# A hybrid decoder step on one core: the sample's state space beside the last projection units, attention's constants awaited where they are read, and the first expert tile's lookup in four parts

## The reference, cut to what matters

```python
proj = rmsnorm(h, g_mix) @ w_in                       # 1024 -> z, xbc, dt, q, k, v
xc = silu(causal_dwconv(concat(conv_buf, xbc), conv_w) + conv_b)
y, ssm_final = ssd_chunked(xs * dt, adt, b, c, ssm0)  # prompt: 8 chunks of 128; sample: one chunk of 4
y_ssm = grouped_rmsnorm((y + d_skip * xs) * silu(z)) * g_ssm_norm
o = diff_attention(q, k_all, v_all, pos0, lam, rel_bias)   # sample: against 2048 cached tokens in pages
h = h + concat(y_ssm, rmsnorm(o, g_diff_norm) * (1 - lam_init)) @ w_out
q = rmsnorm(h) @ w_query                              # 8 heads, two halves of 128
s1, i1 = top_k(q[..0] @ keys0.T, 16); s2, i2 = top_k(q[..1] @ keys1.T, 16)
sc, pos = top_k(s1[:, None] + s2[None, :], 16); idx = (i1 * 128 + i2)[pos]
h = h + sum_k softmax(sc)_k * gelu(u[idx_k] . x) * v[idx_k]      # 128 experts a token
h = h + (p_l @ w_ple) * sigmoid(rmsnorm(h) @ w_ple_gate); y = rmsnorm(h, g_final)
```

## Time and profile before

| | |
|---|---|
| three runs | 3808.51, 3808.66, 3820.09 us; median 3808.66 |
| profiled execution | 3804.01 us; span on the core 3802.4 us |
| PE busy | 2278.3 us (60%), 9714 instructions |
| DVE busy | 2223.9 us (58%), 5285 |
| ACT busy | 1166.0 us (31%), 3659 |
| POOL busy | 1277.7 us (34%), 1247 |
| moved by DMA | 1260.74 MB, 332 GB/s over the span |
| chain that ended last, by engine | DMA 39%, PE 15%, issue 7%, DVE 6%, ACT 6%, POOL 4% |
| the same chain's largest line | the gathers of L2488: 38% |

### The profile page before, as it was taken

How to read it: one execution, slowest core, us unless ns; L and a number is a source line. 1 busy time by engine, 2 the same in 40 slices (tenths; PEclk the granted TensorE clock), 3 DMA queues, 4 the chain that set the end, 5 groups by cost and what they waited for, 6 DMA issues and landing times.

```text
span 3802.4 us, 33311 instructions
## 1 busy us (share of the span) xinstructions
PE 2278.3 (60%) x9714; PEld 775.3 (20%) x9714; DVE 2223.9 (58%) x5285; ACT 1166.0 (31%) x3659; POOL 1277.7 (34%) x1247
## 2 busy tenths in 40 slices
PE   7999934869355456355545635544564563466667
PEld 3555421435011011011101101100110110022211
DVE  4235143543768756855875685586578557645553
ACT  3122113431232422242242223224223322434443
POOL 0000012310244444444434444444444443433332
PEclk9899966989667567566656757666675765677778
DMA  3211027963499999999999999999999999999995
GB/s 102 69 51 57 20 72 266 344 223 121 198 421 421 421 420 421 413 415 421 412 413 419 420 414 410 421 416 407 421 418 413 419 420 412 406 362 391 382 397 213
DMA packets 214609, 1260.74 MB, mean 332 GB/s; under 512 B 27670, under 2 KB 30315, under 8 KB 79043
## 3 DMA queue, kind: packets, MB, share of 16 engines
q0 software_dynamic: 165008, 1147.82, 73.8%
q1 hardware_dynamic: 42122, 93.59, 7.0%
q10 hardware_dynamic: 7296, 17.21, 1.2%
HBM read 1238.80 MB, written 24.25 MB: 332 GB/s over the span
## 4 chain that ended last, share of the span: by engine, by line
DMA 39%; PE 15%; issue 7%; DVE 6%; ACT 6%; POOL 4%; ACTq 1%; POOLq 0%; DVEq 0%; SPq 0%
DMA ex_ring<-in_expert_uv,ex_idx_cur 38%; PE ex_acc L2650 6%; PE ex_pk L2312 4%; POOL ex_ring L2488 4%; DVE ex_ring L2598 2%; ACT ex_diag L2540 2%; ACT ex_coef L2534 2%; PE ex_pt L1896 1%; PE ex_pk L1918 1%; PE ex_pk L2161 1%; PE ex_pk L2324 1%; DMA ex_ring<-in_expert_uv,ex_idx_few 1%; ACT ex_act_out L2531 1%; DVE ex_work L2059 1%; DVE ex_work L2052 1%
## 5 line engine op out<-in xcount | busy, mean ns | idle before, releaser
L2598 DVE CUSTOM_DVE_ANT_0 ex_ring<-ex_ring,ex_rows 128x1024 f32<-128x1024 f32 x1056 | 1292.5, 1225 | 923.0 <-DMA ex_ring<-in_expert_uv,ex_idx_cur 880.4
L2488 POOL DMA_INDIRECT ex_ring<-in_expert_uv,ex_idx_cur x1024 | 1131.9, 1105 | 1690.6 <-PE ex_acc L2650 1370.2
L2650 PE MATMUL ex_acc<-ex_ring,ex_diag 128*32 128x512 f32 x4224 | 866.4, 892 | 1138.9 <-ACT ex_diag L2540 1138.4
L2531 ACT ACTIVATE ex_act_out<-ex_dots 128x2 f32<-128x2 f32 x528 | 108.0, 205 | 1746.8 <-DVE ex_dots L2598 1746.3
L2650 PEld LDWEIGHTS ex_acc<-ex_ring,ex_diag 128*32 128x32 f32 x4224 | 105.8, 129 | 1835.5 <-ACT ex_diag L2540 1762.6
L2540 ACT ACTIVATE ex_diag<-ex_pick_row,ex_coef 128x32 f32<-128x32 f32 x1056 | 283.2, 315 | 49.4 <-ACT ex_coef L2534 1.1
L2534 ACT ACTIVATE ex_coef<-ex_act_out,ex_gate_cur 128x1 f32<-128x1 f32 x1024 | 246.6, 288 | 16.7
L1918 PE MATMUL ex_pk<-ex_w,ex_aT 128*128 128x512 f32 x512 | 250.2, 631 | 0.5 <-DVE ex_aT L1967 0.5
L293 PE MATMUL pj_bank<-pj_aT,pj_wbuf 128*128 128x512 f32 x512 | 226.4, 598 | 0.4 <-ACT pj_aT L408 0.4
L2312 PE MATMUL ex_pk<-ex_w,ex_aT 128*128 128x512 f32 (+1 forms) x288 | 151.2, 677 | 47.0 <-issue 45.2
L1896 PE MATMUL ex_pt<-ex_wo,ex_aT 128*128 128x512 f32 x256 | 131.4, 657 | 5.7 <-ACT ex_aT L1932 5.7
(11 more groups left out here) (377 smaller groups left out, 2497.0 us busy)
## 6 DMA issues: line engine op xcount, KB each, us to landing
at_ring<-in_cache_kT POOLq DMA_DIRECT2D x64, 256.0 KB, 6.4
at_ring<-in_cache_kT SPq DMA_DIRECT2D x64, 256.0 KB, 8.9
at_ring<-in_cache_v SPq DMA_DIRECT2D x64, 256.0 KB, 9.4
at_ring<-in_cache_v POOLq DMA_DIRECT2D x64, 256.0 KB, 6.2
ex_ring<-in_expert_uv,ex_idx_cur POOLq DMA_INDIRECT x1024, 13.3
pj_wbuf<-in_w_in SPq DMA_DIRECT2D x6, 2048.0 KB, 8.5
ex_ring<-in_w_queryT ACTq DMA_DIRECT2D x4, 2048.0 KB, 23.5
pj_front<-in_x_all SPq DMA_DIRECT2D x8, 512.0 KB, 4.4
```

What stands on the lines that cost most here:

```text
L2488: pool.indirect_dma_start(ring[:, c % RING, :], None, t["expert_uv"], bass.IndirectOffsetOnAxis((idx_cur[k % 2] if k < LAST else idx_few)[ ...
L2531: act.activation(act_out[:, half, :], dots[:, half, :], ACT.Gelu).then_inc(gelu_done, 1)
L2598: dve.tensor_tensor_reduce(out=u, in0=u, in1=rows[:, j, :], scale=1.0, scalar=0.0, op0=ALU.mult, op1=ALU.add, accum_out=dots[:, q % HALVES ...
L2650: mm = pe.matmul(acc[n][quarter(j), :], diag[:, q % HALVES, p, :], ring[:, c % RING, D + n * 512:D + (n + 1) * 512], start=False, stop=las ...
```

## The change

1. `ssd` is gone. The sample's state space is spread over the last units of the projection: from unit `FEW` = 52 each engine runs one step (`few_tensor`, `few_scalar`, `few_vector`) behind its part of the unit, in tiles that the projection has done with. SP loads its inputs behind the weights (`few_loads`) and stores the results (`few_stores`). ACT's two convolution copies stand behind k's "few" unit, and the prompt's last `out_vector` in unit 52's step.

```diff
+    FEW = SSD_AT + PT * PHASES
+        def few_stores(sp):
+            sp.wait_ge(f_y_up, 1 + G)
+            sp.dma_start(t["mix"][SEQ:SEQ + DEC, 0:D_SSM], f_y).then_inc(f_stored, 16)
+            for b in range(DEC_B):
+                sp.wait_ge(f_added, b + 1)
+                sp.dma_start(t["ssm_s"][b], f_state[:, b, :]).then_inc(f_stored, 16)
...
+        def few_new(pe, b):
+            if b >= 2:
+                pe.wait_ge(f_added, b - 1)
+            for i in range(G):
+                part = slice(i * HALF, (i + 1) * HALF)
+                mm = pe.matmul(q_new[b % 2][:, part], f_xc[:, D_SSM + i * NS:D_SSM + (i + 1) * NS], f_xdm[:, b, part],
+                               start=True, stop=True)
+            mm.then_inc(f_new, 1)
...
+        def few_tensor(pe, at):
...
+            elif at == 9:
...
+                pe.wait_ge(f_s_in, 32)
+                pe.wait_ge(f_own_up, 1)
+                for i in range(G):
+                    for b in range(DEC_B):
+                        mm = pe.matmul(q_o[:, i * HALF:(i + 1) * HALF], f_cTm[:, b, i, :],
+                                       f_state[:, b, i * HALF:(i + 1) * HALF], start=(b == 0), stop=(b == DEC_B - 1))
+                mm.then_inc(f_off, 1)
+                pe.wait_ge(f_el_up, 1)
+                for b in range(2):
+                    few_new(pe, b)
...
+            elif at >= 10:
+                for b in (2, 3) if at == 10 else range(4, DEC_B):
+                    few_new(pe, b)
...
+        def few_vector(dve, v, at):
...
+            elif at == 10:
+                dve.wait_ge(f_off, 1)
+                v.step(dve.tensor_tensor(heads(f_y), heads(q_o), wide(f_eac[:], few_head), ALU.mult))
+                dve.wait_ge(f_diag, 1)
...
+                dve.tensor_tensor(f_y, f_y, f_z, ALU.mult).then_inc(f_y_up, 1)
+                for b in range(2):
+                    few_add(dve, v, b)
+            elif at == 11:
+                for b in range(2, DEC_B):
+                    few_add(dve, v, b)
...
                 for c in range(2, len(CHUNKS)):
                     weights(c)
+                few_loads(sp)
+                few_stores(sp)
...
+                    if n >= FEW:
+                        few_tensor(pe, n - FEW)
...
-        ssd(nc, t, sample=True)
```

```diff
+            if U == 0:
+                pe.wait_ge(val_in, 16)
...
+            if U < HD:
+                dve.wait_ge(bias_in[U], 16)
...
+        def sample_start(dve, v):
+            dve.wait_ge(sel_in, 16 * 3)
+            dve.wait_ge(consts, 16 * 2)
...
+            dve.wait_ge(s_bias_in, 16 * DEC_S)
...
+                for tok in range(DEC_S):
+                    act.dma_start(s_bias[tok::DEC_S, :],
+                                  bass.AP(t["line"].tensor, X_OFF - PAST - tok, [[0, 8], [LINE, HD], [1, PAST + DEC_S]])
+                                  ).then_inc(s_bias_in, 16)
...
+                    if U == 3:
+                        sample_start(dve, v)
```

```diff
+        def rest_vector(dve, v):
+            for n in range(1, PAIRS):
+                dve.wait_ge(scored, n + 1)
+                for step, _ in enumerate(search(dve, n, v, pk[n], ranked, n + 1, 0)):
+                    if n >= 2 and step == 6:
+                        first_divide(dve, v, n - 1)
+                    yield
+                yield from first_found(dve, v, n)
+            yield from few_vector(dve, v)
...
+                for n in range(4):
+                    src = t["w_queryT"][4 * n * P:4 * (n + 1) * P, :].rearrange("(c p) d -> p c d", p=P)
+                    sp.dma_start(wqT[:, 4 * n:4 * n + 4, :], src).then_inc(wq_in[n], 16)
...
+                        if k == 0 and i % QUADS == 0:
+                            pool.wait_ge(idx0, GRP * GRP * (i // QUADS + 1))
...
-                for n in range(4):
-                    src = t["w_queryT"][4 * n * P:4 * (n + 1) * P, :].rearrange("(c p) d -> p c d", p=P)
-                    act.dma_start(wqT[:, 4 * n:4 * n + 4, :], src).then_inc(wq_in[n], 16)
...
+                rest = rest_vector(dve, v)
+                for _ in range(4):
+                    next(rest)
+                rows_vector(dve, 0, 0)
+                first_divide(dve, v, 0)
+                for j in range(1, GRP):
+                    for _ in range(3):
+                        next(rest)
                     rows_vector(dve, 0, j)
```

More of the change, by code:

```diff
@@ L2123, in few_vector @@
         def few_vector(dve, v):
[L2124 removed]
             dve.wait_ge(few_scored, 1)
[L2126 removed]
+            for step, _ in enumerate(search(dve, 0, v, pk[0], few_ranked, 1, 0)):
+                if step == 6:
+                    first_divide(dve, v, PAIRS - 1)
+                yield
             v.settle()
             dve.tensor_copy(idx_few[:], idx_f[:, 0:QUADS]).then_inc(few_idx, 1)
[L2129 removed]
             dve.tensor_scalar(neg[:, 0:2], best[:, 0:2, 0], -1.0, None, ALU.mult).then_inc(few_negated, 1)
@@ L2137, in few_scalar @@
         def few_scalar(act):
-            yield from pause(33)
             act.wait_ge(few_ranked, 1)
@@ L2144, in few_scalar, with first_found @@
                                accum_out=total[:, h:h + 1]).then_inc(few_grown, 1)
+        def first_found(dve, v, n):
+            v.settle()
+            dve.tensor_scalar(neg[:, 2 * n:2 * n + 2], best[:, 2 * n:2 * n + 2, 0], -1.0, None, ALU.mult).then_inc(negated0, 1)
+            at, end = n * QUADS, (n + 1) * QUADS
+            for j in range(GRP):
+                for q in range(GRP):
+                    dve.tensor_copy(idx_cur[0][quarter(q), at + j:end:GRP], idx_f[quarter(j), at + q:end:GRP]).then_inc(
+                        idx0, 1)
+                yield
@@ new lines, in first_divide, with first_grow @@
+        def first_divide(dve, v, n):
+            two = slice(2 * n, 2 * n + 2)
+            dve.wait_ge(grown0, 2 * (n + 1))
+            v.step(dve.reciprocal(total[:, two], total[:, two]))
+            dve.tensor_tensor(gate_f[:, two], gate_f[:, two], wide(total[:, two], [P, 2, TOPK]), ALU.mult).then_inc(
+                divided0, 1)
+        def first_grow(act, n):
+            act.wait_ge(ranked, n + 1)
+            act.wait_ge(negated0, n + 1)
+            for h in range(2 * n, 2 * n + 2):
+                act.activation(gate_f[:, h, :], best[:, h, :], ACT.Exp, bias=neg[:, h:h + 1],
+                               accum_out=total[:, h:h + 1]).then_inc(grown0, 1)
@@ L2148, in experts, with rest_scalar @@
+        def rest_scalar(act):
+            yield from pause(5)
+            for n in range(1, PAIRS):
+                first_grow(act, n)
+                yield from pause(9)
+                yield from first_gates(act, n)
+                yield from pause(4)
+            few_scalar(act)
         wqT = ring[:].rearrange("p r d -> p (r d)").rearrange("p (c d) -> p c d", d=D)
@@ L2580, in _ @@
                     pass
-                for j in range(groups_of(0)):
+                dve.wait_ge(scored, 1)
+                for _ in search(dve, 0, v, pk[0], ranked, 1, 0):
+                    pass
+                for _ in first_found(dve, v, 0):
+                    pass
+                rest = rest_vector(dve, v)
[6 more added lines that the diff above has]
+                        next(rest)
                     rows_vector(dve, 0, j)
                 for k in range(TILES):
-                    sides = beside(k, lambda n: front_vector(dve, n, v), few_vector(dve, v), lambda n: ends(end_vector, dve, n))
+                    sides = beside(k, lambda n: front_vector(dve, n, v), rest, lambda n: ends(end_vector, dve, n))
                     n = TILE_CALLS[k]
```

704 lines of the change are left out of this document (268 added, 436 removed).

## The result

The changed kernel takes 3715.71 us (median of 4 runs, 3712.74 to 3719.11) against 3810.66 for the kernel before (the three runs shown before and a fourth): a ratio of 0.9749, 95% interval 0.9737 to 0.9761, some 95 us less. The forecast was 3706, with a range of 3692 to 3722. The profiled execution of the changed kernel took 3712.74 us, with a span of 3711.1; that is 91.3 under the span of before.

What follows compares the result with a forecast made beforehand. PE was taken to bound the projection's end and attention, DMA the first expert tile, with gaps between stages removable. Gains 53 + 10 + 40 + 0 = 103 us gave 3706, range 3692 to 3722, about 8 in 10.

Steps and rivals of the forecast that it cites:

- Part 1: Between projection and attention: sample's state space beside v's units, attention starting at 521 instead of 574.5, gain 53 us.
- The wait: Before the last unit, PE's third state pair waits 4.1 us for DVE's y products and first state sum.
- (e): In v's units and attention, TensorE's clock falls to 1.2 GHz: slower, 3850 and up to 3940; chance 0.03.
- Part 2: Attention's start: fewer bias-load issues ahead, so the values become the next late arrival; gain 10 us, likely 6 to 14.
- Part 3: First expert tile's lookup: calls wait for the first search only, first call 45.4 us earlier, 5 lost, gain 40.
- the lag of 19: First expert tile: DVE's first product comes about 19 us behind POOL's first call, 11.0 before.
- The rival with POOL's long calls: First expert tile: POOL's calls go past 2.5 us, so the lookup gains only 20 to 30; chance 0.12.
- Part 4: Expert stage's start: query weights' four loads leave ScalarE's queue for SyncE's; gain 0 us, bounds -2 and 11.
- rival (b): First expert tile: DVE or POOL bounds it, the lookup gives 20 to 30, total 3716 to 3726; chance 0.12.
- (c): Projection's end: the sample's chain stays on the path, the state-space move gives 35, total 3724; chance 0.09.
- (d): Attention's start and first tile: more is hidden, gains of 15 and 45, total 3696; chance 0.08.
- a granted clock below 0.9 in attention's first 50 us: Attention's start: one of the signs listed as showing the forecast wrong.

Runs made afterwards that it cites:

- timed alone: The kernel before with only the sample's state space moved into the projection's last units: 3757.17 us, ratio 0.9865.
- Alone, timed: The kernel before with only attention's constants awaited where they are read: 3800.23 us, ratio 0.9972.
- the three parts timed alone: The kernel before with one changed part each: state space 3757.17 us, attention's constants 3800.23, expert stage 3773.27.
- the two without it: Changed kernel with y's products and first state sums a unit earlier, 3704.46 us; and with that plus four other edits, 3691.79.

## Why the forecast held, and the steps that did not

**Part 1, 53 forecast, 51 found** (timed alone, 45 to 58). The wait was there, in the place that the forecast named and of its size (4.23 for 4.1); DVE's tail took 9.9 for 9.6, the stores and the barrier 8.7 for 7.2, since nine issues take 4.9 and not 3.8. What the forecast left out was the granted clock behind the wait: it had that mechanism as a rival for the whole of v and of attention (e), and it came true over 7.4 us. Unit 63 ended at 504.7 for 502.4. The readout and first pairs were a little cheaper than estimated: unit 62 ended at 493.1, where 483.9 - 1.95 + 12 is 494. (The 15.0 us that the prediction gives for the old readout are 32 times its mean; the records overlap, and the earlier trace rows has them busy for 9.5.) That 53 came so near owes something to luck: taking the upper end of 519 to 521 gave 1.8 us, about half of the 3.5 that the clock took and the sum did not have.

**Part 2, 10 forecast.** The next late arrival, the values, and its time (+37.1 for +38) are right. Alone, timed, the part saves 7 to 14, and the profile of that run does not show it; so 10 is borne out by the timed total, and by the rows only as far as the first product. The 2 us that the set-up gives back were 2.7, since PE's clock also rose later. The prediction reads attention as bound by PE; PE was also kept waiting by cached pages there (9.8 us in the loop before, 15.1 after), and the profile's 40 slices have the DMA engines at nine tenths in the eighth (665 to 760 us) as well as from the twelfth, not the eleventh, on.

**Part 3, 40 forecast, 40 found** (45.6 - 5.6): the lag of 19 was 18.7, lost once and not recovered, as the rows of DMA show. The rival with POOL's long calls did not come: DMA stands at 1.01 with DVE busy nine tenths, and the longest call in the tile is 1.96 us (1.98 before). The prediction ties the long calls to the searches, and that is only half right: before, calls of 1.97 and 1.98 stand 90 and 316 us behind the first call, where DVE searches from 51 to some 80 and from 160 to 284.

**Part 4 was mis-sized: 0 forecast, 3.5 lost.** The step that failed is "with 8 MB more on SyncE's, the output weights' last half megabyte may come 1 to 2 us later". It was 5, and PE waits for the last of them. I took the shares of two queues with little on one of them as a measure of two full ones. From the turns by packet that the Trainium skill gives in DMA: Bandwidth & Descriptors, section "Queues, rings and completion order", the prediction estimated even shares and a landing 20.5 us behind the stage's start (865 for 844.5). The trace agrees in direction and goes further: the last weights let PE start at +24.0, 19.6 us after their issue for 14.4 before, and 14.7 with the second queue held.

**The sum.** 103 was forecast and 95.6 found, and 97.5 by the three parts timed alone: 51 for 53, 11 for 10, and 35 for 40 in the expert stage, of which 3.5 are part 4's. The rest is within the intervals. The total of 3716 for 3706 has 2 us more from a base of 3810.7 in place of 3808.7. The total alone would not tell the forecast from the lower edge of rival (b), 3716 to 3726; the stage's rows do, with 40 kept in part 3. Rivals (c) and (d) did not come, nor (e) but for the 7.4 us above.

**A sign that could not tell.** The prediction called a granted clock below 0.9 in attention's first 50 us a sign of being wrong. It is 0.50 there after the change, and 0.50 in the kernel before as well: the 0.93 of rival (e) is that of the loop alone.

## What to carry to other kernels

Work that is put beside a bound engine costs its instructions and the waits that it brings into that engine's queue, and a wait can cost more than its length: here 4.2 us of wait, and 3.5 us more in the clock behind it. So look at what releases each wait: here DVE only looked at a unit's end that it did not need. When a load changes queues, ask which load on the other queue is awaited first, and hold the later one back. A stage time taken from one profile per kernel can be off by the size of a small term; one part at a time, timed, told here what two profiles could not (11 us saved by attention's part, none of it in its own profile).

## What the runs showed that was not expected

- A wait of 4.23 us in PE's queue, behind more than 60 us of work at a granted clock of 1.00, was followed by 7.4 us at 0.50 in the changed kernel. All seven profiles that have the wait show the last unit's 64 records at 3.64 us, and the two without it 1.96. In five of the nine the clock also fell once around the start of unit 62, where PE had not waited, for 1.5 to 1.7 us.
- 8 MB on one queue put 5 us on the last of 4 MB on another (19.6 us to landing, and 14.7 with the 8 MB held back).
- The loop of the same attention code, with the same loads, took 221 us in one program and 228 to 230 in another, in two profiles of each; the same records on PE took 179 to 180 us there and 182 to 185 here. Chance between executions is not ruled out.
